# Handing layer 0 its input already turned, and laying weight blocks and router tensors out as whole runs

## What is computed

```python
for layer in range(2):
    h = h + mixer(rms_norm(h, mix_norm), w_in, w_out)      # 0: MoBA + retention, 1: dilated windows
    h = h + hier_moe(rms_norm(h, ffn_norm), ...)           # top-1 group, top-2 of its 8 experts
return rms_norm(h, final_norm)

# in the mixers, proj = rms_norm(h) @ w_in, with 3072 columns in both layers
# in the MoE there are 32 experts, each with gate and up (1024 x 512) and down (512 x 1024)
```

## Time and profile before

| | |
|---|---|
| median of three runs | 1111.41 us |
| span of the profiled execution, first to last instruction | 1110.1 us |
| the median lies above that span by | 1.3 us |
| TensorE busy, of the span | 847.7 us (76%) |
| VectorE, ScalarE, GpSimd busy | 380.6, 243.8, 37.6 us |
| mean DMA rate | 397 GB/s |
| core's mean granted TensorE clock | 0.895 |

### The profile page before, as it was taken

How to read it: one execution, slowest core, us unless ns; L and a number is a source line. 1 busy time by engine, 2 the same in 40 slices (tenths; PEclk the granted TensorE clock), 3 DMA queues, 4 the chain that set the end, 5 groups by cost and what they waited for, 6 DMA issues and landing times.

```text
span 1110.1 us, 21758 instructions
## 1 busy us (share of the span) xinstructions
PE 847.7 (76%) x9146; PEld 537.9 (48%) x9146; DVE 380.6 (34%) x926; ACT 243.8 (22%) x622; POOL 37.6 (3%) x63
## 2 busy tenths in 40 slices
PE   9999979856576767576799999797666656676775
PEld 6877735524243434343488776454333324343432
DVE  6888323312121212021288663323211112121212
ACT  5566301100000000000165763111010000000012
POOL 0013100000000000000000211000000000000000
PEclk9999989978887868788999999899787878888888
DMA  9898899999999999999999668999999999999996
GB/s 353 262 389 329 344 401 425 430 428 430 428 427 430 428 428 430 427 427 430 409 386 363 226 268 337 423 426 428 429 428 429 429 428 429 428 429 430 427 427 256
DMA packets 56577, 440.73 MB, mean 397 GB/s; under 512 B 12113, under 2 KB 12625, under 8 KB 31058
## 3 DMA queue, kind: packets, MB, share of 16 engines
q1 hardware_dynamic: 56240, 440.02, 95.5%
q10 hardware_dynamic: 290, 0.07, 0.0%
HBM read 439.03 MB, written 1.05 MB: 396 GB/s over the span
## 4 chain that ended last, share of the span: by engine, by line
DMA 42%; PE 40%; SPq 10%; another core or an unknown queue 3%; DVE 2%; ACT 2%; issue 1%; ACTq 0%; DVEq 0%; POOL 0%; POOLq 0%
DMA ring<-in_w_expert_up 25%; DMA ring<-in_w_expert_down 15%; PE banks L1120 11%; PE banks L1148 4%; PE banks L999 4%; SPq L520 3%; PE banks L1003 3%; PE banks L1000 3%; SPq L468 3%; PE banks L1161 2%; SPq L472 2%; PE banks L1090 2%; PE banks L1216 1%; PE banks L1218 1%; PE banks L1217 1%
## 5 line engine op out<-in xcount | busy, mean ns | idle before, releaser
L1120 PE MATMUL banks<-ring,scratch 128*32 128x256 f32 x4096 | 297.4, 455 | 174.0 <-DMA ring<-in_w_expert_up 173.5
L1120 PEld LDWEIGHTS banks<-ring,scratch 128*32 128x32 f32 x4096 | 152.9, 130 | 313.0 <-issue 175.1
L1632 DVE TENSOR_SCALAR scratch<-scratch 128x128 f32<-128x128 f32 x64 | 14.6, 228 | 618.4 <-ACT scratch L763 605.2
L762 ACT ACTIVATE scratch<-banks 128x128 f32<-128x128 f32 x64 | 17.8, 278 | 573.5 <-PE banks L1120 554.8
L1148 PE MATMUL banks<-ring,h 128*32 128x256 f32 x2048 | 128.0, 390 | 12.8 <-DMA ring<-in_w_expert_down 12.6
L1161 PE MATMUL banks<-h 32*128 32x256 f32 x1024 | 74.4, 403 | 36.5 <-ACT h L772 36.5
L1148 PEld LDWEIGHTS banks<-ring,h 128*32 128x32 f32 x2048 | 62.9, 111 | 58.8 <-issue 25.0
L1161 PEld LDWEIGHTS banks<-h 32*128 32x128 f32 x1024 | 50.2, 187 | 65.8 <-issue 65.8
L999 PE MATMUL banks<-split,h_high 128*128 128x512 f32 x192 | 77.6, 404 | 0.6 <-DVE split L1424 0.2
L1424 DVE SCALAR_TENSOR_TENSOR split<-ring,gains,split 128x512 fp32r<-128x512 f32 x96 | 69.8, 766 | 23.2 <-ACT split L810 22.6
L1003 PE MATMUL banks<-split,h_low 128*128 128x512 f32 x192 | 75.2, 391 | 0.0
(11 more groups left out here) (173 smaller groups left out, 739.0 us busy)
## 6 DMA issues: line engine op xcount, KB each, us to landing
ring<-in_w_expert_gate SPq DMA_DIRECT2D x62, 2048.0 KB, 47.5
ring<-in_w_expert_up SPq DMA_DIRECT2D x61, 2048.0 KB, 48.9
ring<-in_w_expert_down SPq DMA_DIRECT2D x56, 2048.0 KB, 49.2
ring<-in_w_in_even SPq DMA_DIRECT2D x5, 2048.0 KB, 18.1
ring<-in_w_expert_down SPq DMA_DIRECT2D x10, 1024.0 KB, 10.1
ring<-in_w_in_odd SPq DMA_DIRECT2D x5, 2048.0 KB, 19.7
ring<-in_w_expert_up SPq DMA_DIRECT2D x6, 1024.0 KB, 10.8
ring<-in_w_out_even SPq DMA_DIRECT2D x2, 2048.0 KB, 9.0
```

The costliest lines, as they stand in the source:

```text
L1120: last = pe.matmul(psum[6][32 * j:32 * j + 32, 0:2 * P].rearrange("p (a s) -> p a s", a=2), xT[:, c, SLOTS * k:SLOTS * k + SLOTS], ring[:, ...
```

## The change

**x.** The host lays out a second copy of the input, `x_turned`, as 128 partitions x (8 chunks x 256 tokens). SyncE loads it in two halves of 512 KB, in the places in the queue where the rows of x stood, into a part of the ring that is free then (`x_t`). ScalarE and VectorE split it from SBUF, two chunks at a time (`split_x`), in turn with the weight chunks. The 16 transposes of layer 0 go, and the first chunk's six matmuls get an order of their own (`first_product`), which lets four begin before the weight's low part is there. The rows of x are still loaded, for the squares and the residual, now behind block 0 of the weights and ahead of the constants; the squares follow all of block 0's splits.

**Weight blocks.** `w_in` and `w_out` come as blocks of [128, 4096]: a whole block is one run of 16 KB per partition, its pieces are runs of 2, 2, 4 and 8 KB.

**Small tensors.** Six gains come as one tensor `norms` (192 bytes per partition, on ScalarE's queue, ahead of the identity); router weights and biases, padding included, as one tensor `router` of 2.9 KB per partition, behind block 2. Eleven small DMAs of SyncE, two gain loads behind the constants and two memsets go.

```diff
+            def load_x_turned(i):
+                part = slice(C // X_LOADS * i, C // X_LOADS * i + C // X_LOADS)
+                sp.dma_start(x_t[:, part, :], x_turned.rearrange("p (c s) -> p c s", c=C)[:, part, :])\
+                  .then_inc(x_turned_loaded[i], 16)
-            load_x(0)
+            load_x_turned(0)
...
-                    block, source = ring[:, j, :].rearrange("p (c n) -> p c n", c=C), w_in_v[:, :, 512 * b:512 * b + 512]
+                    block, source = (v.rearrange("p (c n) -> p c n", c=C) for v in (ring[:, j, :], w_in[l][b]))
...
                             if l == 0 and i == 0:
-                                load_x(1)
+                                load_x_turned(1)
                         sp.dma_start(block[:, C // 2:, :], source[:, C // 2:, :]).then_inc(w_arrived[j], 16)
                         if l == 0:
+                            for t in range(T):
+                                load_x(t)
                             sp.dma_start(cst[:, P:], consts[:, P:KEPT_CONSTS]).then_inc(const_loaded[1], 16)
-                            for i, g in ((1, ffn_norm[0]), (3, ffn_norm[1])):
-                                load_gain(i, g)
...
+            def split_x(i):
+
+                act.wait_ge(x_turned_loaded[i * X_LOADS // X_PIECES], 16)
+                act.copy(h_high[:, 2 * i:2 * i + 2, :], x_t[:, 2 * i:2 * i + 2, :]).then_inc(h_high_ready, 1)
...
+            def first_product():
+
+                parts = [(psum[t][:, :], h_high[:, 0, P * t:P * t + P], h_low[:, 0, P * t:P * t + P]) for t in range(T)]
+                pe.wait_ge(h_high_ready, 1)
+                pe.wait_ge(w_high_ready, 1)
+                for bank, high, low in parts:
+                    pe.matmul(bank, high, w_high[0], start=True, stop=False)
+                pe.wait_ge(hT_ready, 1)
+                for bank, high, low in parts:
+                    pe.matmul(bank, low, w_high[0], start=False, stop=False)
+                pe.wait_ge(w_low_ready, 1)
+                for bank, high, low in parts:
+                    last = pe.matmul(bank, high, w_low[0], start=False, stop=False)
+                last.then_inc(chunk_used, 1)
...
-            pe.wait_ge(const_loaded[0], 16)
-            for t in range(T):
-                pe.wait_ge(x_loaded[t], 16)
-                for q in range(2):
-                    turn_part(0, t, q)
```

## The result

The changed kernel takes 1116.26 us in the median (1115.00 to 1116.91, four runs), the kernel before 1111.31 in the same comparison. The ratio is 1.0038, with a 95% interval of 1.0026 to 1.0050: it is slower, by 4.2 us in the ratio and 4.95 between the two medians. The profiled execution took 1116.91 us with a span of 1115.0. The median is 3 us above the 1113.2 I forecast, and above the upper end of the range, 1115.6.

The account below looks back on a forecast made before the run. Block 1's landing was taken to time everything behind it: +2.72 us for bytes, -0.53, -0.3 and -0.1 for runs and dropped loads give +1.8 on the 1110.1 span; with 1.3 to the median, 1113.2 us, range 1110.4 to 1115.6.

Parts of the forecast that it names:

- What bounds the kernel: First 30 us: block 1's DMA, landing at 18.64 us, starts VectorE's queue and so times everything behind it.
- the squares would be the next thing late: At the start: squares cost 0 with 1.4 us of cover, but would be late if block 1 came as early as before.
- Bytes ahead of block 1, +2.72: Start of the queue: 1.049 MB more ahead of block 1, at 384 to 386 GB/s, delays its landing by 2.72 us.
- Longer runs, -0.9 in all: Landing of block 1: -0.53 us from its 16 KB runs, -0.3 from block 0's runs, -0.1 from dropped gain loads.
- The sum, +1.8: Landing of block 1: added bytes less longer runs and dropped loads, so about 20.4 us instead of 18.64.
- The lower bound of the sum: Landing of block 1: at least +1.2 us, if the new bytes, block 0 and block 1 all move at 428 GB/s.
- runs bring nothing: Start of the queue: run length does not raise the rate, shift +2.6 to +2.7 us, 1114.1 us; chance 0.14.
- The start of the first product, 6.3 us: TensorE in block 0: first product at 6.3 us instead of 8.42, second chunk at 9.65, gain 0.65 us, idle before block 1.
- The squares, router tensors, layer 1's blocks: 0 each: Squares before block 1, router loads at 40 to 50 us, layer 1's longer runs: each costs or gains 0.
- The seam: Between layer 0's last down pieces and layer 1's blocks: pieces at most 0.4 us faster, taken as 0.
- The clock falls in the new gap: TensorE idle 19.35 to 22.0 us: clock halves, dense matmuls lose 1.7 us, 1113.2 to 1114.9 or more; chance 0.15.
- layer 1 follows the same way: Experts' stream: a shift of TensorE's first expert moves layer 0's end by as much, and layer 1 likewise.

Follow-up runs that it names:

- with 1 MB more: Kernel before plus two 512 KB loads of x into a free place ahead of block 1, nothing else changed: 1114.89 us, ratio 1.0027.
- the changed kernel with filler: Changed kernel plus three filler products on TensorE before each layer's first expert: 1113.50 us, ratio 1.0007 to the kernel before.

## Why the prediction missed, by its own steps

- *What bounds the kernel.* Right in place, not quite in cause. The chain at the start goes through block 1's DMA, and the shift (1.91 us) reaches the first expert nearly undiminished (1.86). The step "the landing of block 1 sets the time of everything behind it" left out the rows of x, whose variance the rotations need just as much. In the kernel before and in the changed one these came early enough. The prediction had said that the squares would be the next thing late, and the two kernels with the rows behind block 1 showed it.
- *Bytes ahead of block 1, +2.72.* Measured by itself: +2.74, or 2.4 to 3.4 with the second profiles of the same starts. Between the changed kernel and the one without x turned it is 2.9 to 3.3.
- *Longer runs, -0.9 in all.* Measured with the blocks alone: -1.0, or -0.35 against the second profile of the same start. The sum, +1.8, came out as +1.91 and, in the second profile, +2.3, so that the first profile's agreement is partly luck. The lower bound of the sum was mis-added: its own numbers, 15.6 and 14.5 us, give +1.1 and not +1.2. The rule of the Trainium skill that I had weighed against this term ("DMA: Bandwidth & Descriptors", "Specifications", line rate from 512 bytes on) does not hold here: in the same stretch, 12 to 18 us, 2 KB runs gave 384 GB/s and the kernel with the blocks alone, where only the runs differ, 430. The rival "runs bring nothing" falls with it.
- *The start of the first product, 6.3 us.* Wrong: 7.38. Weight chunk 0's high part was split at 6.51, not at once after x's, since ScalarE waited 1.10 us for its 256 KB. The gain on TensorE was not 0.65: the second chunk began at 10.02 and not 9.65, and block 0 ended at 20.37, later than the 20.0 of before, with the clock at 0.50 from 8 to 11 us. It cost nothing, because block 1 was later still; the run with a third filler product shows that.
- *The squares, router tensors, layer 1's blocks: 0 each.* Right. The last square ended at 18.1 us and the second variance at 18.3, with block 1 at 20.55. The rate from 40 to 50 us rose from 72 to 422 GB/s with nothing gained, and the kernel without x turned equals the one with the blocks alone.
- *The seam.* Between the first expert and the end of layer 0 0.66 us of the shift was given back; I had put at most 0.4 at the seam and taken 0. The traces put it at layer 0's first experts and not at the seam: 0.96 us goes with the earlier rise of the clock there, less 0.30 lost between the first expert's load and the first down products. (Where both ends can be read, in twelve profiles, the stretch takes 402.6 to 402.7 us with an adding product of 2.09 there, and 401.3 to 402.1 with 1.15 or 1.44.) In the second profile, with the clock as in the kernel before, nothing was given back. From the last down matrix of layer 0 to the first down products of layer 1 it is 147.16 us in both kernels, so layer 1's projections and attention handed the shift on exactly.
- *The clock falls in the new gap.* A rival with the right engine and the wrong place. In the changed kernel's two profiles the gap before block 1 (1.77 us, and none to speak of) left the clock at 1.00. It did fall there with 1 MB more (gap 3.28 us), and in the changed kernel with filler (2.29 us). The sign I had named, a clock under 1.00 anywhere before 100 us, did come, from 8 to 11 us in block 0, and cost nothing. What I did not have at all is a growth of the shift 680 us later.
- **The step that failed is "layer 1 follows the same way".** The prediction let the shift pass through layer 1's experts unchanged, at no cost. It grew there: from 1.20 to 4.94 us in the first profile of the changed kernel, from 2.33 to 4.71 in the second, where with 1 MB more it went from 3.13 to 3.22. One part of it is the clock. The clock falls in the idle time in front of each layer's experts, and how long it stays low varies (until about 702 or 707 us). The rows for it stood in the profile of the kernel before: the earlier trace rows show the clock at 0.50 after such an idle time and back after some 3.4 us of work. I priced that mechanism only where the change makes a gap, not where a gap is met at another moment.

**What stays open.** The cause of the rest of the growth is not shown. The clock behind the first down products isn't all of it, as the profile with the third product at the start has the whole lateness without it. Nor is it shown that the changed kernel meets the late rise more often: of the profiles with x turned two of seven have it, of the others three of seven. Lateness is not the reason by itself, since the kernel with 1 MB more is later at the first expert and loses 2.8 us only. The tail of the stream, four microseconds long in the first profile, was about three in the second and is two to four in the others, and no run took it apart. A rival that no run tests is that the kernels with x turned have one input more, so that the arrays may lie elsewhere in memory; a kernel before with such an unused input would tell. The intervals, some 1.3 us either way for each kernel, leave room for a microsecond from chance as well.

## What to carry to other kernels

Count the bytes ahead of the first transfer that someone waits for: a second copy of an input, loaded to save transposes that lay in idle time, cost its full transfer time here, 1 MB for 2.4 to 3.4 us, while TensorE's saved work was worth nothing. Lay out what is loaded in long runs where it is free to do so; 2 KB runs gave 384 GB/s and 16 KB runs 430 in the same stretch. And where an engine comes out of several idle microseconds, price the clock there before reckoning that a shift passes through unchanged; filler work in the idle time is a cheap test, and here a gain in the changed kernel. Where two kernels differ by a few microseconds, take more than one profile of each: block 1 landed 0.7 us apart in two profiles of the same start, and a stroke of luck in layer 0 hid 1 us of the shift.

## What the runs showed of the hardware that I had not expected

- The granted clock did not follow from an idle time's length alone. After 1.77, 1.88 and 2.32 us of idle TensorE it stayed at 1.00; after 1.87, 2.13, 2.29, 2.54 and 3.28 it fell to 0.50. The 1.87 and the 1.88 stand at the same place, before the first product, in two kernels that are alike up to 140 us.
- 2.7 us of filler, half of the idle time it stood in, gained 3.8 us in the changed kernel (0.34%, give or take 0.16), and at most 1 us in three others, though the clock held through in one of eight places only.
- A DMA stream at 428 GB/s does not end at once. In its last microseconds the rate fell from 377 through 234 and 74 to 29 GB/s in one profile, from 295 through 94 to 0 in another, with the last matrix waited for to the end.
